# Other homes in SBUF for the tensors of a two-block transformer kernel on one core

## The chip, the core and the metric

The kernel runs on one core of a Trainium2 chip. TensorE does the matrix products, ScalarE and VectorE prepare operands and do the pointwise work, GpSimd takes small pieces and a few transfers, and SyncE issues the loads of the weights. The metric is the device time of one execution in microseconds (us); three runs of the kernel before gave 1877.51, 1879.15 and 1881.04 us.

SBUF, the memory on the chip, has 128 partitions. A tensor has the same start address in each partition. That start is called its home here, in bytes of the partition.

## The reference

Two blocks run one after the other on 256 rows of 1024 columns, all in float32. The first has two layers, the second has one. What matters here are the large products:

```python
def first_block(...):
    for l in range(2):
        h = _swiglu(x, ffn_w1[l, 0], ffn_w3[l, 0], ffn_w2[l, 0])      # 1024 -> 2816 -> 1024
        x = _layernorm(ALPHA * x + 0.5 * h, ln_g[l, 0], ln_b[l, 0])
        h = _mixer(x, l, w_in[l], ..., w_branch[l], w_out[l], cos, sin)  # 1024 -> 7168, attention, -> 1024
        x = _layernorm(ALPHA * x + h, ln_g[l, 1], ln_b[l, 1])
        h = _swiglu(x, ffn_w1[l, 1], ffn_w3[l, 1], ffn_w2[l, 1])
        x = _layernorm(ALPHA * x + 0.5 * h, ln_g[l, 2], ln_b[l, 2])
    return x

def second_block(...):
    h = modulate(rmsnorm(x, norm1_g), sh1, sc1)
    z = h @ w_in                                  # 1024 -> 5152, neighbourhood and linear attention
    y = sigmoid(m_a) * (o_na @ w_br_na) + sigmoid(m_b) * (o_gla @ w_br_gla)
    x = x + g1 * (y @ w_out)
    h2 = modulate(rmsnorm(x, norm2_g), sh2, sc2)
    return x + g2 * swiglu(h2, w_ffn_gate, w_ffn_up, w_ffn_down)
```

## The kernel before, in words

**Weights.** SyncE loads the weight matrices in chunks of 1 MB into three buffers `raw`. Each chunk is cut into two parts of 128 by 1024 numbers. ScalarE copies a part from `raw` to one of four buffers `whi` in the type fp32r, which rounds it (L1357), and VectorE writes the remainder `raw - whi` to one of four buffers `wlo` (L1821). The activations are split in the same way into a high and a low tensor.

**Products.** Each product is done as three matmuls: high times high, low times high, high times low. There are two forms.
- `gemm_a` (L671, L672, L674): the weight part is the stationary operand, 128 columns at a time, and the activations are the moving operand, 256 columns (1 KB of a partition). L671 holds `whi` and streams the high activations, L672 holds `whi` and streams the low ones, L674 holds `wlo` and streams the high ones. Each line is issued equally often. A group is eight steps of the contraction, 24 matmuls into one half of a PSUM bank.
- `gemm_b` (L694, L696, L697): the activations are the stationary operand and the weight part is the moving one, 512 columns (2 KB).

**Activations.** In the first block they are in `XTh` and `XTl` for most products, in `HCh` and `HCl` for the products with `w_branch`, and in `ffn1Hh`, `ffn1Hl` (or `ffn3...`) for the second matrix of the feed-forward part. In the second block they are in `HCh` and `HCl` everywhere but for the last matrix, which reads `ffn4Hh` and `ffn4Hl`.

**Order.** The order of every engine's instructions is written out by hand and does not depend on the homes. The queues are: SyncE's for the weights, GpSimd's for biases, tables and small inputs.

**Homes.** `sb` and `some` ask for tensors one after the other, and the allocator lays them down in that order, each size rounded up to 32 bytes, the first one at 16,512 bytes. Tensors in an `ExitStack` that is closed give their place back to the next ones. Worked out from the sizes, these are the starts modulo 1024 bytes, before and after the change:

| tensor | role | before | after |
|---|---|---|---|
| `raw` | landing of the loads | 128 | 0 |
| `whi`, `wlo` | stationary in `gemm_a`, moving in `gemm_b` | 128 | 0 |
| `XTh`, `XTl` | moving in `gemm_a`, stationary in `gemm_b` | 704 | 0 |
| `HCh`, `HCl` | the same, second block and branches | 736 | 0 |
| `ffn1Hh`, `ffn1Hl`, `ffn3Hh`, `ffn3Hl` | stationary in `gemm_b` | 416 | 0 |
| `ffn4Hh`, `ffn4Hl` | moving in `gemm_a` | 192 | 0 |
| `X`, `gb`, `csa`, `c2`, `QNT`, `KNT`, `V2` | attention, norm | 704 | 0 |
| `G2`, `LA`, `VG`, `NP`, `NPT` and others of the second block | attention | 192 | 512 |

Steps inside these tensors are multiples of 512 bytes (a `whi` part in `gemm_a` steps by 512 bytes per contraction step, `XTh` by 1 KB, `HCh` by 2 KB), so the remainder modulo 64 holds for every operand of a product: it was 0 for `whi`, `wlo`, `XTh`, `XTl`, `ffn4Hh`, `ffn4Hl` and 32 for `HCh`, `HCl`, `ffn1Hh`, `ffn1Hl`, `ffn3Hh`, `ffn3Hl`. The distances between a high tensor and its low one stay: 8 KB for `XT`, 16 KB for `HC`, 22 KB for `ffn4`.

Of the kernel before, what the change touches and what calls it, by code (L numbers as in the profile page):

```python
# [9 lines left out]
F32R = mybir.dt.float32r  # L10
# [19 lines left out]
C_ID, C_SHARED, C_CM = 0, 128, 128  # L30
# [320 lines left out]
def program(nc, I, out):  # L351
    ctx = ExitStack()

    def sb(stack, name, shape, dt=F32):
        return stack.enter_context(nc.sbuf_tensor(name, list(shape), dt))

    def some(stack, name, n, shape, dt=F32):
        return [sb(stack, f"{name}{i}", shape, dt) for i in range(n)]
# [4 lines left out]
    with ctx:  # L363
# [20 lines left out]


        bank = [ctx.enter_context(nc.psum_tensor(f"bank{i}", [128, 512], F32)) for i in range(8)]
        raw = some(ctx, "raw", 3, [128, 2048])
        whi = some(ctx, "whi", 4, [128, 1024], F32R)
        wlo = some(ctx, "wlo", 4, [128, 1024], F32R)
        cst = sb(ctx, "cst", [128, C_SHARED])  # L390
        cols = sb(ctx, "cols", [128, 128])
        modc = sb(ctx, "modc", [128, 48, 2])
        c4 = sb(ctx, "c4", [128, 8, 4], F32R)
        spare = sb(ctx, "spare", [128, 512])
        cmb = sb(ctx, "cmb", [4, 2])
        half = sb(ctx, "half", [128, 16])
        XTf = sb(ctx, "XTf", [128, 8, T])
        HCh = sb(ctx, "HCh", [128, 8, 512], F32R)
        HCl = sb(ctx, "HCl", [128, 8, 512], F32R)
        csil = sb(ctx, "csil", [128, 8, 2])  # L400
        sh = sb(ctx, "sh", [128, 48, 2])
        g1c = sb(ctx, "g1c", [128, 8, 2])
        g2c = sb(ctx, "g2c", [128, 8])
        sv2 = sb(ctx, "sv2", [128, 112])
        ident = cst[:, C_ID:C_ID + 128]
        rows = spare[:, 0:128]
        nhalf = half[:, 0:1]

        xst = ExitStack()
# [6 lines left out]
        mv = sb(xst, "mv", [128, 2, 2])  # L416
        rs = sb(xst, "rs", [128, 2, 4])
        gbh = sb(xst, "gbh", [128, 16])
        cm, cos, sin, perm = csa[:, 0:256], csa[:, 256:512], csa[:, 512:768], csa[:, 768:896]

        def ffn_bufs(st, name):
            return (sb(st, name + "Hh", [128, NF, T], F32R), sb(st, name + "Hl", [128, NF, T], F32R),
                    some(st, name + "S", 2, [128, T]), some(st, name + "Hf", 2, [128, T]))
# [64 lines left out]
        with ExitStack() as ns:  # L488
# [3 lines left out]
            NPT = some(ns, "NPT", 2, [128, 512])  # L492
            nv = some(ns, "nv", 3, [128, 8])
        with ExitStack() as fs:
            ffn4 = ffn_bufs(fs, "ffn4")
            OUT = sb(fs, "OUT", [128, 2, D])
        st.close()
# [2136 lines left out]
```

## Time and profile before

| | |
|---|---|
| three runs | 1877.51, 1879.15, 1881.04 us |
| the profiled execution | 1877.37 us, its span 1875.6 us |
| TensorE matmul busy | 1846.2 us, 98% of the span |
| VectorE busy | 1124.1 us, 60% |
| ScalarE busy | 890.9 us, 47% |
| loads | 330.58 MB, mean 176 GB/s |

The profiled execution lasted 1.8 us more than its span, the time from the first to the last instruction. The record of a matmul is longer than the distance to the next one, since matmuls are pipelined. So the busy time of TensorE says little. The pace is read from the distance between starts: in a stretch without a gap it is (length of the stretch + length of one record) / number of records that touch the stretch.

### The profile page before, as it was taken

To read this page: it belongs to the slowest core of one execution; us is meant where nothing else is said; L and a number is where in the kernel's file an instruction comes from. 1 tells how busy PE (TensorE), PEld (TensorE's weight loads), DVE (VectorE), ACT (ScalarE), POOL (GpSimd) and SP (SyncE) were. 2 spreads that over 40 slices of the span, in tenths; PEclk is the share of its full clock that TensorE was granted. 3 is DMA by queue.
4 is the path that set the end of the run, shared out by engine and by line. 5 is a ranking of instruction groups with operands and counts; after the bars stand their busy time and mean duration, and the time that the engine had idled before them with its cause. 6 is when DMAs were issued, how large, how long until landed. Compare 5 with 4: busy or idle time off the path is not lost.

```text
span 1875.6 us, 31147 instructions
## 1 busy us (share of the span) xinstructions
PE 1846.2 (98%) x12859; PEld 1649.6 (88%) x12859; DVE 1124.1 (60%) x1703; ACT 890.9 (47%) x1437; POOL 246.2 (13%) x261
## 2 busy tenths in 40 slices
PE   9999999999999999999999999999998999999999
PEld 8998699999899879986898997999776787879999
DVE  5654586676665465655675776566653645565553
ACT  5553344663455434543435753555344345454443
POOL 1000232111200020001321212000110712100000
PEclk9999999999999999999999999999998999999999
DMA  8665655445666566754745455665444223356553
GB/s 282 193 201 192 227 180 167 148 149 189 203 189 213 184 203 193 231 203 157 254 156 178 136 180 200 214 215 180 157 130 129 90 81 101 113 165 192 183 181 112
DMA packets 252397, 330.58 MB, mean 176 GB/s; under 512 B 13162, under 2 KB 213072, under 8 KB 252256
## 3 DMA queue, kind: packets, MB, share of 16 engines
q1 hardware_dynamic: 248240, 315.31, 52.3%
q0 software_dynamic: 4016, 13.27, 2.1%
q8 instruction: 102, 1.67, 0.4%
q14 instruction: 39, 0.32, 0.1%
HBM read 327.51 MB, written 1.05 MB: 175 GB/s over the span
## 4 chain that ended last, share of the span: by engine, by line
PE 64%; issue 23%; DVE 5%; DMA 3%; POOL 2%; ACT 2%; SPq 1%; DVEq 0%; POOLq 0%; ACTq 0%
PE bank L671 15%; PE bank L672 15%; PE bank L674 15%; PE bank L694 4%; PE bank L696 4%; PE bank L697 4%; DMA G<-in_lam_dram 1%; DVE X L1893 1%; DVE wlo L1821 1%; PE bank L1227 1%; DMA raw<-in_w_in_dram 1%; SPq L640 1%; POOL rs L2416 1%; PE bank L1205 1%; ACT whi L1357 1%
## 5 line engine op out<-in xcount | busy, mean ns | idle before, releaser
L1821 DVE TENSOR_TENSOR wlo<-raw,whi 128x1024 fp32r<-128x1024 f32 (+1 forms) x557 | 686.4, 1238 | 427.7 <-ACT whi L1357 424.9
L1357 ACT ACTIVATE whi<-raw 128x1024 fp32r<-128x1024 f32 (+1 forms) x569 | 594.4, 1051 | 430.3 <-PE bank L674 179.7
L671 PE MATMUL bank<-XTh,whi 128*128 128x256 f32 x2048 | 581.1, 284 | 2.0 <-DVE XTl L1830 2.0
L672 PE MATMUL bank<-XTl,whi 128*128 128x256 f32 x2048 | 572.3, 279 | 0.0
L674 PE MATMUL bank<-XTh,wlo 128*128 128x256 f32 x2048 | 571.9, 279 | 0.0
L671 PEld LDWEIGHTS bank<-XTh,whi 128*128 128x128 f32 x2048 | 384.3, 188 | 7.1 <-DVE XTl L1830 2.7
L672 PEld LDWEIGHTS bank<-XTl,whi 128*128 128x128 f32 x2048 | 384.6, 188 | 1.4
L674 PEld LDWEIGHTS bank<-XTh,wlo 128*128 128x128 f32 x2048 | 383.8, 187 | 0.0
L671 PE MATMUL bank<-HCh,whi 128*128 128x256 f32 (+1 forms) x936 | 272.9, 292 | 8.0 <-ACT whi L1357 5.8
L674 PE MATMUL bank<-HCh,wlo 128*128 128x256 f32 (+1 forms) x936 | 268.4, 287 | 0.0
L672 PE MATMUL bank<-HCl,whi 128*128 128x256 f32 (+1 forms) x936 | 268.0, 286 | 0.0
L671 PEld LDWEIGHTS bank<-HCh,whi 128*128 128x128 f32 x936 | 177.1, 189 | 25.6 <-issue 11.5
L672 PEld LDWEIGHTS bank<-HCl,whi 128*128 128x128 f32 x936 | 176.9, 189 | 2.1
L674 PEld LDWEIGHTS bank<-HCh,wlo 128*128 128x128 f32 x936 | 176.0, 188 | 2.8 <-DVE wlo L1821 0.8
L2416 POOL TENSOR_TENSOR rs<-rs,half 128x1 f32<-128x1 f32 x12 | 18.3, 1525 | 674.2 <-DVE rs L1887 674.2
L697 PE MATMUL bank<-whi,ffn1Hl 128*128 128x512 f32 x264 | 104.4, 396 | 0.0
L694 PE MATMUL bank<-whi,ffn1Hh 128*128 128x512 f32 x264 | 104.4, 395 | 0.0
L696 PE MATMUL bank<-wlo,ffn1Hh 128*128 128x512 f32 x264 | 104.4, 395 | 0.0
L694 PE MATMUL bank<-whi,XTh 128*128 128x512 f32 x192 | 76.2, 397 | 0.0
L697 PE MATMUL bank<-whi,XTl 128*128 128x512 f32 x192 | 75.8, 395 | 0.0
L696 PE MATMUL bank<-wlo,XTh 128*128 128x512 f32 x192 | 75.8, 395 | 0.0
L697 PEld LDWEIGHTS bank<-whi,ffn1Hl 128*128 128x128 f32 x264 | 49.6, 188 | 12.0
(329 smaller groups left out, 2316.0 us busy)
## 6 DMA issues: line engine op xcount, KB each, us to landing
raw<-in_ffn_w_dram SPq DMA_DIRECT2D x131, 1024.0 KB, 5.3
raw<-in_w_in_dram SPq DMA_DIRECT2D x76, 1024.0 KB, 5.2
raw<-in_w_mod_dram SPq DMA_DIRECT2D x24, 1024.0 KB, 5.1
raw<-in_w_branch_dram SPq DMA_DIRECT2D x16, 1024.0 KB, 5.1
raw<-in_w_out_dram SPq DMA_DIRECT2D x12, 1024.0 KB, 5.0
raw<-in_w_ffn_gate_dram SPq DMA_DIRECT2D x11, 1024.0 KB, 5.3
raw<-in_w_ffn_up_dram SPq DMA_DIRECT2D x11, 1024.0 KB, 5.3
raw<-in_w_ffn_down_dram SPq DMA_DIRECT2D x8, 1024.0 KB, 5.2
```

The lines of the kernel that those rows point to most:

```text
L640: e.dma_start(BT[64 * j:64 * j + 64, h, :, :], src).then_inc(BIAS[h].did(h, by=16), 16)
L671: e.matmul(o, hi[:, k, w0:w0 + nc_], xh, start=first and k == 0, stop=False)
L672: e.matmul(o, hi[:, k, w0:w0 + nc_], xl, start=False, stop=False)
L674: m = e.matmul(o, lo[:, k, w0:w0 + nc_], xh, start=False, stop=last and k == nk - 1)
L694: e.matmul(o[:, :], xh, hi[:, k, s], start=kk == 0, stop=False)
L696: e.matmul(o[:, :], xh, lo[:, k, s], start=False, stop=False)
L697: m = e.matmul(o[:, :], xl, hi[:, k, s], start=False, stop=kk == nparts * nk - 1)
L1205: e.matmul(bank[b][:, :], QNT[r, h // 2, t * 128:(t + 1) * 128], KNT[r, h // 2, :], start=True, stop=True).then_inc(SMALL.did(("ns", u)), 1)
L1227: m = e.matmul(o, V2[:, j, h * 64:(h + 1) * 64], NPT[u % 2][:, j * 128:(j + 1) * 128], start=j == 0, stop=j == 3)
L1357: e.activation(hi_part(n), raw_part(n), ACTF.Copy).then_inc(WHI.did(n), 1)
L1821: e.tensor_tensor(lo_part(n), raw_part(n), hi_part(n).bitcast(F32), ALU.subtract).then_inc(WLO.did(n), 1)
L2416: e.tensor_tensor(rs[:, t, 1:2], rs[:, t, 0:1], nhalf, ALU.pow).then_inc(PLN.did(("rs", j, t)), 1)
```

## The change

The order in which the shared tensors are asked for is another. `cst` and `modc` (896 bytes together) come first and fill the way up to 17,408 bytes, which is 17 KB. Then follow `raw`, `whi`, `wlo`, `XTf`, `HCh`, `HCl` and `spare`, whose sizes are multiples of 1 KB, then the small ones. Three tensors that nobody reads or writes (`gap0` 320 bytes, `gap1` 272, `gap2` 512) pad up to the next multiple of 1 KB ahead of `X`, of the buffers of the first block's stages, and of `ffn4`. Nothing else changes: the lists of instructions of all engines are the same, row for row, but for the line numbers, which grow by 2 to 4 behind the edits.

```diff
@@ -384,24 +384,26 @@
         bank = [ctx.enter_context(nc.psum_tensor(f"bank{i}", [128, 512], F32)) for i in range(8)]
+
+        cst = sb(ctx, "cst", [128, C_SHARED])
+        modc = sb(ctx, "modc", [128, 48, 2])
         raw = some(ctx, "raw", 3, [128, 2048])
         whi = some(ctx, "whi", 4, [128, 1024], F32R)
         wlo = some(ctx, "wlo", 4, [128, 1024], F32R)
-        cst = sb(ctx, "cst", [128, C_SHARED])
-        cols = sb(ctx, "cols", [128, 128])
-        modc = sb(ctx, "modc", [128, 48, 2])
-        c4 = sb(ctx, "c4", [128, 8, 4], F32R)
-        spare = sb(ctx, "spare", [128, 512])
-        cmb = sb(ctx, "cmb", [4, 2])
-        half = sb(ctx, "half", [128, 16])
         XTf = sb(ctx, "XTf", [128, 8, T])
         HCh = sb(ctx, "HCh", [128, 8, 512], F32R)
         HCl = sb(ctx, "HCl", [128, 8, 512], F32R)
+        spare = sb(ctx, "spare", [128, 512])
+        cols = sb(ctx, "cols", [128, 128])
+        sh = sb(ctx, "sh", [128, 48, 2])
+        c4 = sb(ctx, "c4", [128, 8, 4], F32R)
+        half = sb(ctx, "half", [128, 16])
         csil = sb(ctx, "csil", [128, 8, 2])
-        sh = sb(ctx, "sh", [128, 48, 2])
         g1c = sb(ctx, "g1c", [128, 8, 2])
         g2c = sb(ctx, "g2c", [128, 8])
         sv2 = sb(ctx, "sv2", [128, 112])
+        cmb = sb(ctx, "cmb", [4, 2])
+        sb(ctx, "gap0", [128, 80])
@@ -416,6 +418,7 @@
         gbh = sb(xst, "gbh", [128, 16])
+        sb(xst, "gap1", [128, 68])
@@ -492,6 +495,7 @@
         with ExitStack() as fs:
+            sb(fs, "gap2", [128, 128])
             ffn4 = ffn_bufs(fs, "ffn4")
```

## Rows read from the trace of the kernel before

**Rows 1.** The page: engines, busy us, share, instructions; then the granted clock.
```profile
PE 1846.2 (98%) x12859; PEld 1649.6 (88%) x12859; DVE 1124.1 (60%) x1703; ACT 890.9 (47%) x1437; POOL 246.2 (13%) x261
PEclk9999999999999999999999999999998999999999
```

**Rows 2.** The page: the chain that ended last, by engine, then by line.
```profile
PE 64%; issue 23%; DVE 5%; DMA 3%; POOL 2%; ACT 2%; SPq 1%; DVEq 0%; POOLq 0%; ACTq 0%
PE bank L671 15%; PE bank L672 15%; PE bank L674 15%; PE bank L694 4%; PE bank L696 4%; PE bank L697 4%; DMA G<-in_lam_dram 1%; DVE X L1893 1%; DVE wlo L1821 1%; PE bank L1227 1%; DMA raw<-in_w_in_dram 1%; SPq L640 1%; POOL rs L2416 1%; PE bank L1205 1%; ACT whi L1357 1%
```

**Rows 3.** Waits of the PE engine: total us, times, longest us.
```profile
PE bank L671 <- ACT whi L1357: 5.8, 1, 5.8
PE bank L696 <- DVE wlo L1821: 3.8, 2, 3.1
PE bank L732 <- DVE X L1893: 3.1, 5, 0.7
...
PE bank L732 <- DMA X<-in_x_dram: 1.1, 1, 1.1
...
PE bank L1152 <- DVE QD L2204: 0.9, 1, 0.9
```

**Rows 4.** Instruction groups by form: shape, count, busy us, mean ns, idle before.
```profile
L671 PE MATMUL bank<-XTh,whi 128*128 128x256 f32 x2048 | 581.1, 284 | 2.0 <-DVE XTl L1830 2.0
...
L671 PE MATMUL bank<-HCh,whi 128*128 128x256 f32 x912 | 261.4, 287 | 2.2 <-DVE HCl L2242 1.7 <-DVE tmp L2306 0.4
...
L694 PE MATMUL bank<-whi,ffn1Hh 128*128 128x512 f32 x264 | 104.4, 395 | 0.0
...
L694 PE MATMUL bank<-whi,XTh 128*128 128x512 f32 x192 | 76.2, 397 | 0.0
...
L671 PE MATMUL bank<-ffn4Hh,whi 128*128 128x256 f32 x176 | 49.5, 281 | 0.0
```

**Rows 5.** Stretches: us, busy (x records) per engine, granted clock, DMA share, GB/s.
```profile
500.00:550.00 50.00, 50.00 (x427) 50.00 (x426) 27.90 (x35) 24.35 (x36) 0.00 (x0) 1.00 0.61 191
1180.00:1220.00 40.00, 40.00 (x342) 40.00 (x341) 23.27 (x29) 20.10 (x29) 0.00 (x0) 1.00 0.65 204
1700.00:1800.00 100.00, 100.00 (x836) 100.00 (x835) 56.70 (x71) 49.36 (x71) 0.00 (x0) 1.00 0.58 182
1105.00:1125.00 20.00, 20.00 (x169) 20.00 (x169) 13.45 (x20) 9.88 (x13) 4.99 (x6) 1.00 0.59 201
1830.00:1865.00 35.00, 35.00 (x300) 35.00 (x299) 16.18 (x17) 13.52 (x15) 0.00 (x0) 1.00 0.41 130
150.00:200.00 50.00, 50.00 (x216) 40.24 (x215) 22.52 (x22) 17.47 (x18) 0.00 (x0) 1.00 0.56 189
```

**Rows 6.** Timeline of PE, one group of XTh: 21 matmuls lie between these two.
```profile
361.32 0.28 PE L672 MATMUL bank<-XTl,whi 128*128 128x256 f32 x1
...
363.81 0.28 PE L674 MATMUL bank<-XTh,wlo 128*128 128x256 f32 x1
```

**Rows 7.** A stretch of 512-column matmuls on HCh at half clock.
```profile
1425.00:1427.00 2.00, 2.00 (x6) 1.58 (x5) 1.97 (x4) 1.95 (x4) 0.29 (x1) 0.50 0.73 193
```

**Rows 8.** Timeline of PE there: 8 matmuls of 512 columns lie between these two.
```profile
1423.75 0.63 PE L671 MATMUL bank<-HCh,whi 128*128 128x512 f32 x1
...
1427.59 0.58 PE L671 MATMUL bank<-HCh,whi 128*128 128x512 f32 x1
```

**Rows 9.** Groups by form: one operation on ffn1 (home 416) and ffn4 (home 192).
```profile
L1853 DVE TENSOR_TENSOR ffn1Hl<-ffn1Hf,ffn1Hh 128x256 fp32r<-128x256 f32 x66 | 28.1, 425 | 31.9 <-ACT ffn1Hh L1391 31.9
...
L1391 ACT ACTIVATE ffn1Hh<-ffn1Hf 128x256 fp32r<-128x256 f32 x66 | 27.6, 418 | 39.2 <-DVE ffn1Hf L1850 39.2
...
L1853 DVE TENSOR_TENSOR ffn4Hl<-ffn4Hf,ffn4Hh 128x256 fp32r<-128x256 f32 x22 | 9.4, 425 | 10.6 <-ACT ffn4Hh L1391 10.6
...
L1391 ACT ACTIVATE ffn4Hh<-ffn4Hf 128x256 fp32r<-128x256 f32 x22 | 9.2, 418 | 11.9 <-DVE ffn4Hf L1850 11.9
```

**Rows 10.** DMA issues: count, size, median us from issue to landing.
```profile
raw<-in_ffn_w_dram SPq DMA_DIRECT2D x131, 1024.0 KB, 5.3
```

## Prediction

> **What bounds the kernel now.** I read the page first: TensorE's records cover 98% of the span, VectorE's 60%, ScalarE's 47%, at a clock that is at its upper level (2.4 GHz) nearly throughout [rows 1]. Then the chain: 64% of it is TensorE and 23% is "issue", and the three lines of `gemm_a` and the three of `gemm_b` lead it [rows 2]. Then the waits of TensorE: the longest is 5.8 us, and the others are a few us each [rows 3]. So the time is the number of matmuls times their distance, and a change of homes matters if it changes that distance. The instruction lists are the same, so no wait is added or taken away by the program.
>
> **The distance between matmuls.** All stretches used here have matmuls without a gap, and I divide (stretch + one record) by the records.
> - `XTh`, `XTl` streamed, 256 columns: (50 + 0.28) / 427 = 117.75 ns and (40 + 0.28) / 342 = 117.78 ns [rows 5].
> - `HCh`, `HCl` streamed, 256 columns: (100 + 0.28) / 836 = 119.95 ns and (20 + 0.28) / 169 = 120.0 ns [rows 5]. The first is in the second block, the second in the first block's branch products, so it isn't the stage.
> - `ffn4Hh`, `ffn4Hl` streamed: (35 + 0.28) / 300 = 117.6 ns [rows 5].
> - `whi`, `wlo` streamed, 512 columns: (50 + 0.395) / 216 = 233.3 ns [rows 4, 5].
>
> At 2.4 GHz, 256 columns are 106.7 ns and 512 are 213.3 ns. So each kilobyte costs some 10 to 13 ns more than its columns. At the lower clock this extra is gone: nine steps in 3.84 us are 426.7 ns, exactly 512 columns at 1.2 GHz [rows 7, 8]. I conclude that at the upper clock the reading of the operands sets the distance, and not the array. That makes the homes worth a look. The pace isn't set by transfers or other engines: 130 GB/s and 204 GB/s, ScalarE busy 39% and 50% of the stretch, give the same 117.6 to 117.8 ns [rows 5].
>
> The records themselves show the same difference: 284 ns for `XTh`, 281 for `ffn4Hh`, 287 for `HCh` [rows 4].
>
> **The change part by part.**
>
> *The streamed `HCh`, `HCl` (home 736, after 0).* What sets them apart from `XT` (704) and `ffn4` (192) is that they start at 32 modulo 64 bytes, where the others start at 0. The distance from the high to the low tensor does not sort them: it is 8 KB for one fast pair and 22 KB for the other. Nor does the stationary operand, which is `whi` or `wlo` at 128 in all. After the change they start at a multiple of 64. I take for them the pace of `XT`: 119.95 - 117.75 = 2.2 ns less per matmul. They are 912 on each of three lines [rows 4], 2736 in all: 2736 x 2.2 ns = 6.0 us. Not all of it reaches the end. Two groups (48 matmuls) run ahead of the 5.8 us wait for `whi`, whose part comes from a load, and four groups (96) run ahead of the 0.9 us wait for `QD` [rows 3]. A faster TensorE only waits longer there: 144 x 2.2 ns = 0.3 us is lost. That leaves 5.7 us. Bounds: nothing, if the 32 bytes aren't the reason; and 2736 x (119.95 - 113.2) = 18.5 us, if they fall to the best pace that the trace has (below).
>
> *The streamed `XT` and `ffn4` (704 and 192, after 0).* 3 x 2048 + 3 x 176 = 6672 matmuls. Both homes are 192 modulo 512, so the trace has only one start of this form at the good pace, and a start at 0 modulo 512 isn't shown. The nearest row says 117.75 ns, and I take no change. The bounds are wide. One group of `XTh` runs at (363.81 - 361.32) / 22 = 113.2 ns [rows 6], at the same addresses as all the others. In the timeline I count ten such groups of 256, all among the gates of the two mixers (361 to 389 and 1040 to 1069 us), each behind small matmuls of the attention; the other 246 are at 117.8. So a group falls into one of two rhythms by how it starts, and keeps it. Another home could tip all of them either way: 6672 x (117.75 - 113.2) = 30.4 us less, or, at the pace of `HC`, 6672 x 2.2 = 14.7 us more.
>
> *The streamed `whi`, `wlo` in `gemm_b` (128, after 0).* 233.3 ns whether the stationary operand is `ffn1` (home 416, 32 modulo 64) or `XT`: the records are 395 and 397 ns [rows 4]. At 512 columns the stationary home doesn't count, and the moving one already starts at a multiple of 128 bytes. I take nothing. Bound: the part that depends on the operand reading is 233.3 - 213.3 = 20 ns on each of some 1970 matmuls (264 and 192 on each of three lines [rows 4], and some 200 more on each), but no row has a 512-column stream at the upper clock without it, so I keep nothing for it beyond the tails.
>
> *Stationary operands.* In `gemm_a` the `whi` slices step by 512 bytes, so half of them started at 128 and half at 640, and go to 0 and 512. In the timeline the pace does not alternate with them. Nothing.
>
> *ScalarE, VectorE, GpSimd.* The same operations on `ffn1` (32 modulo 64) and `ffn4` (0) take 418 and 418 ns, 425 and 425 ns [rows 9]. Nothing, and both have idle time in any stretch [rows 5].
>
> *Loads.* `raw` moves from 128 to 0. A chunk of 1 MB lands 5.3 us after its issue [rows 10], and a chunk is used up in 48 x 117.75 ns = 5.65 us, with three buffers. If landing changed by a tenth either way, 0.5 us would show at the two waits that end with a load, for `X` (1.1 us) and for `whi` (5.8 us) [rows 3]: at most 1 us more or less. I take nothing. At `HC`'s new pace a chunk is needed every 5.65 us instead of 5.76, which `XT` stretches already bear.
>
> **The sum.** 1877.37 us (the profiled execution) - 5.7 = 1871.7 us. The median of the three runs lies 1.8 us above the profiled execution, which would make it 1873.4. I say 1872.
>
> **The Trainium skill against it.** The trace shows 120.0 ns for starts at 32 modulo 64 and 117.75 for starts at 0 modulo 64 [rows 5]. The Trainium skill, "SBUF — State Buffer", section "Specifications (TRN2)", gives lines of 16 bytes that need two hits or more for full bandwidth. By that rule every home before was at the start of a line already, a run of floats hits each line four times, and the change is worth nothing: 1877.4. It does not explain the 2.2 ns, so I follow the row, but it is one reason for the chance that I leave to no effect. The Trainium skill, "TensorE: Matmul & The Clock Gate", section "Step-by-step: what each phase is for", says that moving and stationary operands come through two independent read ports. By that rule an equal start of both operands cannot hurt, and rival three falls away. The two rhythms at one set of addresses [rows 6] speak for some coupling, and no row tells whether it is this one.
>
> **The rivals.**
> 1. *No effect.* `HC` is slow for another reason than the 32 bytes, for instance that its pair is 16 KB apart, just as `whi` and `wlo` are, or that its slices step by 2 KB. All this stays. Against it: the product rows show no other common trait of `XT` and `ffn4`. Time: 1877.4.
> 2. *The fast rhythm everywhere.* With both operands at full kilobytes all 256-column groups run at 113.2 ns. For it: the rhythm exists at unchanged addresses [rows 6]. Against it: no back-to-back group has it. Time: 1877.4 - 30.4 - 18.5 = 1828.5.
> 3. *Slower: the two operands of a matmul meet.* Before, moving and stationary starts differed by 64 modulo 512 for `XT` (704 - 128 = 576) and `ffn4` (192 - 128 = 64), and by 96 for `HC`. After, they differ by 0 everywhere. If both reads then fall on the same place at the same time, `XT` and `ffn4` go to the slow rhythm of 119.95 ns and `HC` stays: 1877.4 + 14.7 = 1892.1. It decides wherever 256-column groups run back to back, from the first feed-forward part on. For it: the difference sorts the streams as well as the 32 bytes do. Against it: its order is not monotone in any way that I can read.
>
> **How the numbers follow.** The forecast gets 0.50, no effect 0.19, the fast rhythm 0.17, the slower one 0.14. The forecast's own range is 1868 to 1875. The range for 8 in 10 holds the forecast, no effect and the slower rival, and leaves out the fast rhythm (0.17): 1864 to 1893. About 0.2%, 3.8 us, can be told from no change by a measurement of this kernel. Faster by more: 0.47 of the forecast's 0.50 and all of the fast rhythm, 0.64. Within: 0.03 and 0.19, 0.22. Slower: 0.14.
>
> **What would show it.** Right: stretches of `HC` at 117.8 ns, that is 851 records in a stretch of 100 us instead of 836, and the record of `HCh` 3 ns shorter; 427 records in 50 us of `XT` as before; 216 in 50 us of the 512-column form. The records of ScalarE and VectorE keep their means. The forecast is wrong if `HC` stays at 836 (first rival), if `XT` goes to 444 (second) or to 419 (third), or if the 512-column form leaves 233.3 ns, which none of my cases has.

## The result, and the profile after: slower by 0.23%

The changed kernel takes 1882.75 us (median of 13 runs, 1880.81 to 1884.3), the one before 1878.0 us (13 runs, 1875.0 to 1881.04). The ratio is 1.0023, with a 95% interval of 1.0015 to 1.0032: slower, by little more than a measurement can tell. I had forecast 1872 us. The time lies in my range and the sign is wrong. Of all the timed executions in this document one, of the kernel w128 below, took 2225.67 us at a granted clock of 0.75, and no ratio includes it.

The profiled span is 1881.5 us (before 1875.6). Lines behind the edits are 4 higher, so `gemm_a` is L675, L676 and L678, and `gemm_b` is L698, L700 and L701. The page's first line and the shares of its chain are those of [rows 1, 2] but for a point:

```profile
PE 1849.3 (98%) x12859; PEld 1664.8 (88%) x12859; DVE 1125.6 (60%) x1703; ACT 890.5 (47%) x1437; POOL 245.4 (13%) x261
...
PE 64%; issue 23%; DVE 5%; DMA 3%; POOL 2%; ACT 2%; SPq 1%; DVEq 0%; POOLq 0%; ACTq 0%
```

What moved is in the groups of instructions with their shapes (busy time, then the mean of one in ns):

```profile
L675 PE MATMUL bank<-XTh,whi 128*128 128x256 f32 x2048 | 589.4, 288 | 2.0 <-DVE XTl L1834 2.0
...
L675 PE MATMUL bank<-HCh,whi 128*128 128x256 f32 x912 | 262.6, 288 | 2.2 <-DVE HCl L2246 1.7 <-DVE tmp L2310 0.4
...
L698 PE MATMUL bank<-whi,ffn1Hh 128*128 128x512 f32 x264 | 102.7, 389 | 0.0
...
L698 PE MATMUL bank<-whi,XTh 128*128 128x512 f32 x192 | 75.2, 392 | 0.0
...
L675 PE MATMUL bank<-ffn4Hh,whi 128*128 128x256 f32 x176 | 50.1, 284 | 0.0
```

The streamed activations are longer (`XTh` 284 to 288 ns, `ffn4Hh` 281 to 284, `HCh` 287 to 288), the streamed weights shorter (395 to 389 on `ffn1`, 397 to 392 on `XTh`) [rows 4]. A record holds more than the distance to the next, so the size is read from counts: records of TensorE in a stretch without a gap. The rows are `XT`, `HC`, the 512-column form on `ffn1`, and `ffn4`:

```profile
500.00:550.00 50.00, 50.00 (x419) 50.00 (x418) 27.92 (x35) 24.01 (x34) 0.00 (x0) 1.00 0.58 184
1700.00:1780.00 80.00, 80.00 (x669) 80.00 (x669) 45.17 (x56) 39.10 (x56) 0.00 (x0) 1.00 0.59 185
150.00:190.00 40.00, 40.00 (x178) 33.14 (x177) 17.81 (x15) 15.66 (x15) 0.00 (x0) 1.00 0.58 192
1825.00:1850.00 25.00, 25.00 (x211) 25.00 (x210) 13.04 (x14) 9.42 (x11) 0.00 (x0) 1.00 0.60 192
```

(Stretch + one record) / records gives 50.28 / 419 = 120.0 ns for `XT` (before 117.75), 80.28 / 669 = 120.0 for `HC` (before 119.95), 40.39 / 178 = 226.9 for the 512-column form (before 233.3), 25.28 / 211 = 119.8 for `ffn4` (before 117.6) [rows 5]. One record more or less makes 0.3 ns in 50 us of `XT`, 0.6 ns in 25 us of `ffn4` and 1.3 ns in 40 us of the 512-column form. So both signs of being wrong have come: 419 records in 50 us, which I had named for my third rival, and 512-column matmuls off 233.3 ns, which I had said none of my cases has.

The three longest waits of TensorE stand in the same order as before, and the wait for `G` has moved up to the fourth place:

```profile
PE bank L675 <- ACT whi L1361: 6.9, 1, 6.9
PE bank L700 <- DVE wlo L1825: 4.0, 2, 3.3
PE bank L736 <- DVE X L1897: 3.9, 5, 0.8
...
PE bank L844 <- POOL G L2432: 2.2, 2, 1.6
```

The first three were 5.8, 3.8 and 3.1 us [rows 3]. The one for `G` was 1.1 us:

```profile
PE bank L840 <- POOL G L2428: 1.1, 2, 0.6
```

**Where the time went**, as number times change of distance:

| stream | matmuls | ns each | us |
|---|---|---|---|
| `XT`, 256 columns | 6144 | +2.25 | +13.8 |
| the ten groups that ran at 113.2 ns | 240 | +4.5 beyond that | +1.1 |
| `ffn4`, 256 columns | 528 | +2.2 | +1.2 |
| `HC`, 256 columns | 2736 | 0 | 0 |
| weights on `ffn1`, `ffn3`, 512 columns | 1056 | -6.6 | -7.0 |
| weights on `XT`, 512 columns | 576 | -6.4 | -3.7 |
| weights on `HC`, 512 columns | 336 | about -8 | -2.7 |
| waits for `whi`, for `G` and for `X` | | | about +3 |

They add up to some +6, and the spans differ by 5.9 us. The row on `HC` with 512 columns is read from the starts of its matmuls in both traces, where 84.5 us became 81.8; the mean change there holds more than the pace, since few of these matmuls run long without a break. The rows come from one profiled execution of each, and the runs of a kernel spread by 3 to 6 us, so I don't press the last microsecond. Two effects of opposite sign nearly cancel: +16 us on 256 columns and -13 us on 512.

ScalarE and VectorE keep their durations, as forecast [rows 9]:

```profile
L1395 ACT ACTIVATE ffn1Hh<-ffn1Hf 128x256 fp32r<-128x256 f32 x66 | 27.6, 418 | 36.5 <-DVE ffn1Hf L1854 36.5
...
L1857 DVE TENSOR_TENSOR ffn1Hl<-ffn1Hf,ffn1Hh 128x256 fp32r<-128x256 f32 x66 | 28.1, 425 | 31.9 <-ACT ffn1Hh L1395 31.9
```

### The profile page after: what moved, and what is told of

It reads as the page before. It is cut to its first block, busy times and chain, and to the rows that moved or that the text cites. A ratio compares the mean times of both kernels' runs of the same rounds, so it can differ in the third digit from the quotient of the medians.

```text
span 1881.5 us, 31147 instructions
## 1 busy us (share of the span) xinstructions
PE 1849.3 (98%) x12859; PEld 1664.8 (88%) x12859; DVE 1125.6 (60%) x1703; ACT 890.5 (47%) x1437; POOL 245.4 (13%) x261
## 4 chain that ended last, share of the span: by engine, by line
PE 64%; issue 23%; DVE 5%; DMA 3%; POOL 2%; ACT 2%; SPq 1%; DVEq 0%; POOLq 0%; ACTq 0%
PE bank L675 15%; PE bank L678 15%; PE bank L676 15%; PE bank L698 4%; PE bank L700 4%; PE bank L701 4%; DMA G<-in_lam_dram 1%; DVE X L1897 1%; DMA raw<-in_w_in_dram 1%; DVE wlo L1825 1%; PE bank L1231 1%; SPq L644 1%; POOL rs L2420 1%; ACT whi L1361 1%; PE bank L1209 1%
## 5 line engine op out<-in xcount | busy, mean ns | idle before, releaser
L675 PE MATMUL bank<-XTh,whi 128*128 128x256 f32 x2048 | 589.4, 288 | 2.0 <-DVE XTl L1834 2.0
L676 PE MATMUL bank<-XTl,whi 128*128 128x256 f32 x2048 | 579.9, 283 | 0.0
L678 PE MATMUL bank<-XTh,wlo 128*128 128x256 f32 x2048 | 579.9, 283 | 0.0
L675 PEld LDWEIGHTS bank<-XTh,whi 128*128 128x128 f32 x2048 | 392.2, 191 | 7.1 <-DVE XTl L1834 2.7
L676 PEld LDWEIGHTS bank<-XTl,whi 128*128 128x128 f32 x2048 | 392.2, 192 | 1.4
L678 PEld LDWEIGHTS bank<-XTh,wlo 128*128 128x128 f32 x2048 | 392.2, 191 | 0.0
L675 PE MATMUL bank<-HCh,whi 128*128 128x256 f32 (+1 forms) x936 | 274.2, 293 | 9.1 <-ACT whi L1361 6.9
L678 PE MATMUL bank<-HCh,wlo 128*128 128x256 f32 (+1 forms) x936 | 269.1, 288 | 0.0
L676 PE MATMUL bank<-HCl,whi 128*128 128x256 f32 (+1 forms) x936 | 269.0, 287 | 0.0
L675 PEld LDWEIGHTS bank<-HCh,whi 128*128 128x128 f32 x936 | 179.8, 192 | 27.2 <-issue 12.1
L678 PEld LDWEIGHTS bank<-HCh,wlo 128*128 128x128 f32 x936 | 179.6, 192 | 2.7 <-DVE wlo L1825 0.8
L676 PEld LDWEIGHTS bank<-HCl,whi 128*128 128x128 f32 x936 | 180.0, 192 | 2.1
L698 PE MATMUL bank<-whi,ffn1Hh 128*128 128x512 f32 x264 | 102.7, 389 | 0.0
L700 PE MATMUL bank<-wlo,ffn1Hh 128*128 128x512 f32 x264 | 102.7, 389 | 0.0
L701 PE MATMUL bank<-whi,ffn1Hl 128*128 128x512 f32 x264 | 102.7, 389 | 0.0
L698 PE MATMUL bank<-whi,XTh 128*128 128x512 f32 x192 | 75.2, 392 | 0.0
L700 PE MATMUL bank<-wlo,XTh 128*128 128x512 f32 x192 | 74.8, 390 | 0.0
L701 PE MATMUL bank<-whi,XTl 128*128 128x512 f32 x192 | 74.7, 389 | 0.0
L1393 ACT ACTIVATE ffn1S<-bank 128x256 f32<-128x256 f32 x66 | 25.3, 384 | 77.0 <-PE bank L678 77.0
```

Source lines behind the costliest of these rows:

```text
L675: e.matmul(o, hi[:, k, w0:w0 + nc_], xh, start=first and k == 0, stop=False)
L676: e.matmul(o, hi[:, k, w0:w0 + nc_], xl, start=False, stop=False)
L678: m = e.matmul(o, lo[:, k, w0:w0 + nc_], xh, start=False, stop=last and k == nk - 1)
L698: e.matmul(o[:, :], xh, hi[:, k, s], start=kk == 0, stop=False)
L700: e.matmul(o[:, :], xh, lo[:, k, s], start=False, stop=False)
L701: m = e.matmul(o[:, :], xl, hi[:, k, s], start=False, stop=kk == nparts * nk - 1)
```

## The experiments

Theory B of the recorded expectations: the distance between matmuls follows from the *difference* of the two homes that one matmul reads, start of the streamed operand minus start of the held one, modulo some power of two (512 in the first expectations, 256 in the later ones). My own theory of the prediction (A) was that the streamed home alone counts. All kernels below change homes only: the order in which tensors are asked for, and tensors that nobody uses as padding. "Home" is the start modulo 1024 bytes. Before: weights 128, `XT` 704, `HC` 736, `ffn1` and `ffn3` 416, `ffn4` 192. `raw`, `whi` and `wlo` always start alike, but in one kernel.

**w0** puts the weights at 0 and leaves the activations at 704, 736, 416 and 192. **w128** does the reverse: weights stay at 128, the activations go to 0.

```diff
 (w0, against before)
+        cst = sb(ctx, "cst", [128, C_SHARED])
+        modc = sb(ctx, "modc", [128, 48, 2])
         raw = some(ctx, "raw", 3, [128, 2048])
         whi = some(ctx, "whi", 4, [128, 1024], F32R)
         wlo = some(ctx, "wlo", 4, [128, 1024], F32R)
-        cst = sb(ctx, "cst", [128, C_SHARED])
+        XTf = sb(ctx, "XTf", [128, 8, T])
         cols = sb(ctx, "cols", [128, 128])
-        modc = sb(ctx, "modc", [128, 48, 2])
...
 (w128, against before)
...
         gbh = sb(xst, "gbh", [128, 16])
+        sb(xst, "pad2", [128, 72])
...
+            sb(fs, "pad4", [128, 208])
             ffn4 = ffn_bufs(fs, "ffn4")
```

> Only the weight parts move: raw, whi, wlo start at 0 modulo 1024 as after the change, XT stays at 704, HC at 736, ffn1 and ffn3 at 416, ffn4 at 192 as before it. Theory A (the pace of a matmul depends on the start of its moving operand alone): 256-column matmuls as before, 117.8 ns on XT and ffn4 and 120.0 on HC; 512-column matmuls, which stream the weight parts, 226.7 ns as after. Time 1878.0 - 12 = 1866 us. Theory B (it depends on the difference of the two starts): XT - weights was 64 modulo 512 and is 192, so XT leaves 117.8, and the 512-column matmuls have three new differences (416, 704, 736) and would not all run at 226.7. Time 1876 to 1893 us.

> The other half of the change: the weight parts stay at 128 as before, XT, HC, ffn1, ffn3, ffn4 start at 0. Theory A (own start of the moving operand): all 256-column matmuls 120.0 ns, 512-column ones 233.3 ns, time 1878.0 + 15 = 1893 us. Theory B (difference of the starts, here 384 modulo 512 for all): the 256-column pace is something else than 120.0, or the 512-column pace something else than 233.3.

w0: 1852.21 against 1878.94 us, ratio 0.9852 (0.9836 to 0.9868). w128: 1880.77 us, ratio 1.001 (1.0 to 1.0019). No time expected for w0 came true: A had 1866 us and B 1876 to 1893. Nor did A's 1893 us for w128. In w0 the stretches of `XT`, `HC` and the 512-column form on `ffn1` are

```profile
480.00:545.00 65.00, 65.00 (x576) 65.00 (x575) 38.12 (x47) 33.82 (x48) 0.00 (x0) 1.00 0.69 222
1700.00:1780.00 80.00, 80.00 (x678) 80.00 (x677) 45.79 (x57) 39.44 (x56) 0.00 (x0) 1.00 0.59 186
150.00:190.00 40.00, 40.00 (x173) 32.16 (x172) 17.15 (x14) 15.63 (x15) 0.00 (x0) 1.00 0.58 192
```

and in w128

```profile
500.00:550.00 50.00, 50.00 (x423) 50.00 (x423) 28.49 (x35) 24.70 (x35) 0.00 (x0) 1.00 0.57 175
1700.00:1780.00 80.00, 80.00 (x676) 80.00 (x676) 45.54 (x56) 39.66 (x58) 0.00 (x0) 1.00 0.60 185
150.00:190.00 40.00, 40.00 (x174) 32.43 (x173) 17.24 (x15) 15.21 (x15) 0.00 (x0) 1.00 0.54 185
```

`XT` has not moved in w0 and goes from 117.75 to 65.28 / 576 = 113.3 ns, which is the fast rhythm of [rows 6], now in some 220 of its 256 groups. `HC` hasn't moved either and goes from 119.95 to 80.28 / 678 = 118.4 ns. The 512-column form, which streams the weights that moved, stays at 40.39 / 173 = 233.5 ns, where A asked for 226.7. So the held operand's home counts, and A is out. In w128 the home of `HC` is a multiple of 64, and it doesn't take 117.75 ns but 80.28 / 676 = 118.8. In the changed kernel, with the same home 0 and the weights at 0, it took 120.0. Both homes count.

**s1, s2** tell apart a difference and two separate effects. The homes are these: s1 has weights 0, `XT` 64, `HC` 128, `ffn1` 32; s2 has weights 64, `XT` 64, `HC` 128, `ffn1` 0. The edits are paddings and an order near that of the changed kernel. The paddings in the first block, of s1:

```diff
 (s1, against before)
         gb = sb(xst, "gb", [128, 2, D])
+        sb(xst, "pad1", [128, 96])
         XTh = sb(xst, "XTh", [128, 8, T], F32R)
...
         gbh = sb(xst, "gbh", [128, 16])
+        sb(xst, "pad2", [128, 64])
...
```

> Sweep, weight parts at 0. XT at 64, HC at 128, ffn4 at 512, ffn1 and ffn3 at 32. Theory A: 512-column matmuls stay at 226.7 ns whatever the stationary start; the 256-column pace is read for three new starts; 512 (ffn4) should equal 0 and give 120.0 if the pattern repeats every 512 bytes, and 64 or 128 should give 117.8 if it is the distance from such a boundary that helps. Theory B: XT has the difference 64 that it had before, so it runs at 117.8; the 512-column pace differs between ffn1 (difference 32) and XT (64).

> Sweep, weight parts at 64. XT at 64, HC at 128, ffn4 at 256, ffn1 and ffn3 at 0. Theory A: XT (64) and HC (128) run at the same pace as in the run with weight parts at 0 and the same homes; the 512-column pace is that of a stream that starts at 64, a new value between 226.7 and 240. Theory B: XT (difference 0) runs at 120.0, HC (difference 64) at 117.8, and both differ from the other sweep.

Both are single executions: 1876.6 and 1878.44 us. Stretches of s1, then of s2:

```profile
500.00:550.00 50.00, 50.00 (x427) 50.00 (x426) 28.17 (x35) 24.11 (x35) 0.00 (x0) 1.00 0.62 191
1700.00:1780.00 80.00, 80.00 (x676) 80.00 (x676) 45.54 (x56) 39.40 (x56) 0.00 (x0) 1.00 0.59 186
```

```profile
500.00:550.00 50.00, 50.00 (x419) 50.00 (x419) 27.94 (x35) 24.11 (x34) 0.00 (x0) 1.00 0.60 183
1700.00:1780.00 80.00, 80.00 (x681) 80.00 (x681) 46.08 (x58) 39.72 (x57) 0.00 (x0) 1.00 0.60 185
150.00:190.00 40.00, 40.00 (x176) 32.84 (x175) 18.28 (x15) 14.82 (x14) 0.00 (x0) 1.00 0.57 197
```

`XT` at home 64 has 427 records with the weights at 0 (difference 64) and 419 with the weights at 64 (difference 0). 427 is the count of before, where the homes were 704 and 128, and the difference 64 as well modulo 256. `HC` in s2 has difference 64 too, at 80.28 / 681 = 117.9 ns; in s1 it has 128 and 118.8 ns, w128's value at its difference 128. The third row of s2, 512 columns with weights minus held at 64, has 40.39 / 176 = 229.5 ns, where 224 and 192 had 233.3 and 0 had 226.9. The difference sorts all of them.

**best** sets what the rows so far make the best: difference 192 for all 256-column streams, and 0 for the weights on `ffn1` and `ffn3`. **shift32** is best with every home 32 bytes further, so that nothing starts at a multiple of 64 and all differences stay.

```diff
 (best, against w0)
-        cols = sb(ctx, "cols", [128, 128])
         c4 = sb(ctx, "c4", [128, 8, 4], F32R)
         half = sb(ctx, "half", [128, 16])
-        g2c = sb(ctx, "g2c", [128, 8])
         HCh = sb(ctx, "HCh", [128, 8, 512], F32R)
         HCl = sb(ctx, "HCl", [128, 8, 512], F32R)
         spare = sb(ctx, "spare", [128, 512])
+        cols = sb(ctx, "cols", [128, 128])
...
+        g2c = sb(ctx, "g2c", [128, 8])
...
         gbh = sb(xst, "gbh", [128, 16])
+        sb(xst, "pad1", [128, 152])
 (shift32, against best)
         modc = sb(ctx, "modc", [128, 48, 2])
+        g2c = sb(ctx, "g2c", [128, 8])
...
         gb = sb(xst, "gb", [128, 2, D])
+        sb(xst, "pad1", [128, 8])
...
```

> Weight parts at 0, XT at 704, HC and ffn4 at 192, ffn1 and ffn3 at 0 modulo 1024. Theory B (the pace depends on the moving start minus the stationary start, modulo 256): 256-column matmuls have 192 everywhere and run at 113.3 ns, HC too (it was 118.3 with weight parts at 0 and HC at 736); the 512-column ones on ffn1 and ffn3 have 0 and run at 226.7 (233.3 there). Against the kernel with only the weight parts moved, 1852 us: 2661 x 5.0 ns = 12 us and 1048 x 6.7 ns = 7 us less, about 1833 us. Theory A (own start of the moving operand): HC goes to what 192 gave in ffn4, also 113.3, but the 512-column pace cannot depend on the home of ffn1 and stays 233.3: about 1840 us.

> All homes of the kernel with weight parts at 0, XT at 704, HC and ffn4 at 192, ffn1 and ffn3 at 0 moved up by 32 bytes, so that nothing starts at a multiple of 64 and all differences stay. Theory B (differences alone): the same paces, 113.3 ns and 226.7 ns on ffn1. The step of my prediction (32 modulo 64 costs 2.2 ns): 256-column matmuls 2 ns or more longer on all of XT, HC and ffn4.

best: 1839.86 us (1832.58 to 1844.64) against 1879.02, ratio 0.9793 (0.9765 to 0.9821). It is faster than before, by 2.1% (1.8 to 2.4). Against the changed kernel, not timed beside it, the medians give 1839.86 / 1882.75 = 0.977. shift32: 1836.71 us, one execution. In best, an early stretch of `XT`, a later one, `HC`, and the 512-column form:

```profile
480.00:545.00 65.00, 65.00 (x576) 65.00 (x575) 38.73 (x49) 35.12 (x49) 0.00 (x0) 1.00 0.63 202
...
680.00:735.00 55.00, 55.00 (x469) 55.00 (x469) 31.83 (x40) 27.80 (x40) 0.00 (x0) 1.00 0.61 190
...
1700.00:1780.00 80.00, 80.00 (x708) 80.00 (x707) 47.62 (x58) 41.20 (x59) 0.00 (x0) 1.00 0.58 184
150.00:190.00 40.00, 40.00 (x179) 33.10 (x178) 17.48 (x15) 14.85 (x14) 0.00 (x0) 1.00 0.57 187
```

and in shift32 `HC` and the 512-column form:

```profile
1700.00:1780.00 80.00, 80.00 (x708) 80.00 (x707) 47.04 (x58) 40.06 (x57) 0.00 (x0) 1.00 0.62 195
150.00:190.00 40.00, 40.00 (x178) 33.12 (x177) 18.11 (x15) 14.85 (x14) 0.00 (x0) 1.00 0.58 189
```

`HC` runs at 80.28 / 708 = 113.4 ns in both, 6.6 ns below the changed kernel. That no home of these operands is a multiple of 64 in shift32 costs nothing in these rows. The rows of `XT` in best show the two rhythms at one difference: 65.28 / 576 = 113.3 ns, and 55.28 / 469 = 117.9 ns over a stage. In the timeline 77 of `XT`'s 256 groups take the slow one in best, 40 in shift32, 34 to 36 in w0. Against w0 the 43 or so more slow groups are 43 x 24 x 4.44 ns = 4.6 us. Of `HC`'s 114 groups 17 are slow in best as well, another 17 x 24 x 4.44 ns = 1.8 us, and the waits are some 1.3 us longer. That is most of the 8.4 us by which the profiled execution (1841.45 us) misses the 1833 us that were expected. The runs of best spread over 12 us; whether that is the number of slow groups, one trace can't say. Back to back, a group nearly always keeps the rhythm of the one before it, so that most stages go one way; but in the first stage of w0 the fifth group changes and the eleven behind it stay slow. What picks the rhythm is open.

**nextld** asks whether what counts is the operand held *now* or the one being loaded for the next matmul. It is best with `wlo` at 64 and `XTl` at 768, so that the two differences of a matmul, to its own and to the next held operand, part.

```diff
 (nextld, against best)
         whi = some(ctx, "whi", 4, [128, 1024], F32R)
+        sb(ctx, "pad1", [128, 16])
         wlo = some(ctx, "wlo", 4, [128, 1024], F32R)
...
+        sb(xst, "pad2", [128, 240])
         XTh = sb(xst, "XTh", [128, 8, T], F32R)
+        sb(xst, "pad3", [128, 16])
         XTl = sb(xst, "XTl", [128, 8, T], F32R)
...
```

> As the kernel with weight parts at 0, XT at 704, HC and ffn4 at 192, ffn1 and ffn3 at 0, but wlo starts at 64 and XTl at 768, each 64 bytes further; whi and XTh stay. Theory N (a stream meets the load of the NEXT matmul's stationary operand, which runs beside it): the stream of XTl meets the load of wlo, difference 192 modulo 256, the two streams of XTh meet loads of whi, 192 too, so all three of XT stay at 113.3 ns; on HC and ffn4, whose low tensor did not move, the matmul that streams the low tensor gets 128 and takes longer, the other two stay. Theory O (a stream meets its OWN stationary operand): the low stream of XT has 0 and the high one with wlo 128, so XT goes to about 118 ns in the mean; on HC and ffn4 the matmul with wlo gets longer, the one that streams the low tensor doesn't.

1877.61 us, one execution: all of the gain is gone.

```profile
500.00:550.00 50.00, 50.00 (x425) 50.00 (x424) 28.47 (x34) 23.56 (x33) 0.00 (x0) 1.00 0.60 190
1700.00:1780.00 80.00, 80.00 (x679) 80.00 (x679) 45.52 (x56) 39.91 (x57) 0.00 (x0) 1.00 0.60 187
150.00:190.00 40.00, 40.00 (x175) 32.34 (x174) 17.22 (x15) 15.28 (x15) 0.00 (x0) 1.00 0.56 185
```

`XT` is at 118.3 and `HC` at 118.2 ns. From the paces measured above, the own held operand (theory O) asks for (113.3 + 120.0 + 118.8) / 3 = 117.4 ns on `XT` and (113.3 + 113.3 + 118.8) / 3 = 115.1 ns on `HC`. The next one (theory N) asks for 113.3 and 115.1. N fails clearly on `XT`, and both are some 3 ns short on `HC`. On `ffn1` either would have (226.7 + 226.7 + 229) / 3 = 227.5 ns, and the row has 40.39 / 175 = 230.8. So the paces don't add up over the three matmuls of a step: differences that change from one matmul to the next cost more than their mean. Which of the two held operands counts stays open.

**s3** and **s4** read the table at more differences: s3 has weights 0, `XT` 32, `HC` 160, `ffn1` 256, `ffn4` 448. s4 has weights 0, `ffn1` 0, `ffn4` 32, and puts `XT` at 688 and `HC` at 208 by beginning 16 bytes inside a larger tensor.

```diff
 (s4, against w0)
...
-        XTh = sb(xst, "XTh", [128, 8, T], F32R)
-        XTl = sb(xst, "XTl", [128, 8, T], F32R)
+        sb(xst, "pad1", [128, 240])
+        XTb = sb(xst, "XT", [128, 16 * T + 8], F32R)[:, 4:4 + 16 * T].rearrange("p (k t) -> p k t", k=16)
+        XTh, XTl = XTb[:, 0:8, :], XTb[:, 8:16, :]
...
 (s3, against w0)
...
+        sb(xst, "pad1", [128, 88])
         XTh = sb(xst, "XTh", [128, 8, T], F32R)
...
```

> Sweep of the difference, weight parts at 0: XT 32, HC 160, ffn4 448; ffn1 and ffn3 at 256. Theory B with period 256: ffn4 (448 = 192 + 256) at 113.3 ns, ffn1 (difference 0 modulo 256) at 226.7 ns, the 512-column XT (224) at 233.3; XT at 32 and HC at 160 are new points, expected between 113.3 and 120. With period 512 instead, ffn4 and ffn1 differ from that.

> Finer sweep in steps of 16 bytes, weight parts at 0: XT at 688 (difference 176 modulo 256), HC at 208, ffn4 at 32, ffn1 and ffn3 at 0. 192 had two rhythms, 113.3 and 117.8 ns; the question is whether 176 or 208 hold the fast one in all groups. The theory of differences expects ffn4 at 116.8 (what XT had at 32) and ffn1 at 226.7, and XT and HC between 113.3 and 118.5; over 118.5 would be against it.

One execution each: 1866.77 and 1879.56 us. In s3 `XT` (in a good stretch; from 500 to 550 us it has 419 records, which is 120.0 ns), `HC`, `ffn4`, and the 512-column form:

```profile
1180.00:1220.00 40.00, 40.00 (x345) 40.00 (x344) 23.95 (x30) 20.77 (x30) 0.00 (x0) 1.00 0.58 183
1700.00:1780.00 80.00, 80.00 (x677) 80.00 (x676) 45.73 (x57) 39.43 (x57) 0.00 (x0) 1.00 0.59 185
1825.00:1850.00 25.00, 25.00 (x223) 25.00 (x222) 13.37 (x15) 10.46 (x11) 0.00 (x0) 1.00 0.45 146
150.00:190.00 40.00, 40.00 (x178) 33.15 (x177) 18.36 (x15) 15.22 (x15) 0.00 (x0) 1.00 0.59 200
```

and in s4 `XT`, `HC` and `ffn4`:

```profile
500.00:550.00 50.00, 50.00 (x422) 50.00 (x421) 28.25 (x35) 24.62 (x34) 0.00 (x0) 1.00 0.57 180
1700.00:1780.00 80.00, 80.00 (x673) 80.00 (x673) 45.52 (x56) 39.33 (x57) 0.00 (x0) 1.00 0.58 185
1825.00:1850.00 25.00, 25.00 (x217) 25.00 (x216) 12.23 (x13) 9.66 (x11) 0.00 (x0) 1.00 0.68 220
```

s3 sets the modulus at 256: `ffn4` at 448 runs at 25.28 / 223 = 113.4 ns, as at 192, and the 512-column form on `ffn1` at 256 at 40.39 / 178 = 226.9 ns, as at 0. In s4 `XT` at difference 176 takes 50.28 / 422 = 119.1 ns, and `HC` at 208 takes 80.28 / 673 = 119.3 ns. I had written that more than 118.5 would speak against the theory of differences with a cost that falls evenly toward 192, and it does speak against the even fall. These are also the only two homes off the multiples of 32 bytes, so nothing tells whether the differences 176 and 208 are dear or the odd 16 bytes.

**xt640, hc704, ffn128** change one home of the kernel before each: `XT` from 704 to 640 (difference 64 to 0), `HC` from 736 to 704 (96 to 64, which is just the step that my forecast rests on), `ffn1` and `ffn3` from 416 to 128 (weights minus `ffn1` from 224 to 0).

```diff
 (xt640)
+        sb(xst, "pad1", [128, 240])
         XTh = sb(xst, "XTh", [128, 8, T], F32R)
         XTl = sb(xst, "XTl", [128, 8, T], F32R)
+        sb(xst, "pad2", [128, 16])
 (hc704)
-        cmb = sb(ctx, "cmb", [4, 2])
         half = sb(ctx, "half", [128, 16])
...
         g2c = sb(ctx, "g2c", [128, 8])
+        cmb = sb(ctx, "cmb", [4, 2])
 (ffn128)
         gbh = sb(xst, "gbh", [128, 16])
+        sb(xst, "pad1", [128, 184])
```

> The kernel before with XTh and XTl alone moved from 704 to 640, so that their difference to the weight parts (128) is 0 modulo 256, as after the whole change. The theory of differences: XT at 120.0 ns instead of 117.8 (6144 matmuls, +14 us), the 512-column matmuls that hold XT at 226.7 ns instead of 233.3 (576, -4 us), all others as before: about 1889 us against 1879. If instead the start at a full kilobyte were what hurts, 640 would do as well as 704 and nothing would change.

> The kernel before with HCh and HCl alone moved from 736 to 704: the step that I predicted by itself (-5.7 us). The theory of differences: 576 - that is 64 modulo 256, the difference that XT has in the kernel before - gives 117.8 ns on 2736 matmuls instead of 120.0, so 6 us less, 1873 us against 1879, and nothing in the 512-column form. If HC is slow for a reason of its own (pair 16 KB apart, steps of 2 KB), nothing changes.

> The kernel before with the stack of ffn1 and ffn3 alone moved from 416 to 128, so that the 512-column matmuls that stream whi and wlo over them have the difference 0. The theory of differences: 226.7 ns instead of 233.3 on 1056 matmuls, 7 us less, about 1872 us. If the stationary home does not count, as my prediction had it, no change.

| kernel | time, us | ratio to before | 95% interval |
|---|---|---|---|
| xt640 | 1887.83 | 1.0044 | 1.003 to 1.0058 |
| hc704 | 1873.03 | 0.9966 | 0.9955 to 0.9978 |
| ffn128 | 1871.6 | 0.9961 | 0.9948 to 0.9974 |

The times that theory B had named were 1889, 1873 and 1872 us. Each kernel moves its own stream, with one side effect: in hc704 13 of the 20 groups of `ffn4`, whose homes stayed, ran in the fast rhythm, which is worth 1.5 us in its trace. The `XT` stretch of xt640, the `HC` stretch of hc704 and the 512-column stretch of ffn128:

```profile
500.00:550.00 50.00, 50.00 (x419) 50.00 (x419) 28.23 (x34) 24.35 (x34) 0.00 (x0) 1.00 0.56 178
```

```profile
1700.00:1780.00 80.00, 80.00 (x682) 80.00 (x681) 45.67 (x57) 39.78 (x57) 0.00 (x0) 1.00 0.60 185
```

```profile
150.00:190.00 40.00, 40.00 (x178) 33.15 (x177) 18.30 (x15) 15.28 (x15) 0.00 (x0) 1.00 0.59 200
```

They are 120.0, 117.7 and 226.9 ns. xt640 alone costs +9.6 us by the medians (1887.83 - 1878.21) and 0.44%, which is 8.3 us, by the ratio (5.6 to 10.9). ffn128 alone gives 6.6 us by the medians and 0.39%, 7.3 us, by the ratio, for the 1056 matmuls x 6.6 ns = 7.0 us of the table. These are the main parts of the two halves of the change. By the same sum xt640 ought to cost 13.8 + 1.1 = 14.9 us less a gain on its 512-column form, whose difference goes to 0 too (-3.7 us): 11.2, just above that interval. Its own trace has +13.5 and -3.5 us there, 10.0 in all.

## Why the prediction was wrong, step by step

- **What bounds the kernel** held: no wait appeared or went, and the time followed the distance between matmuls. So did the method of counting records. The clause that the reading of the operands sets the distance, and not the array, fits all that follows, but no run shows it.
- **The step on `HC` failed.** I read from two homes that a start at 32 modulo 64 bytes costs 2.2 ns and a start at 0 doesn't. I sorted by the streamed home alone and dismissed the weights with "whi or wlo at 128 in all". They were at 128 in all, and for that reason no row could tell a home from a difference. Against the first rival I wrote that the rows show no other common trait of `XT` and `ffn4`, and the third rival then names one. The difference of `HC` was 96, that of `XT` and `ffn4` 64. shift32 shows that 32 modulo 64 costs nothing. hc704, the step by itself, gave -0.34%, which is 6.4 us (5.2 by the medians), where I had 5.7, and in its trace the matmuls on `HC` take 5.7 us less: right in size by luck, for another reason. The change put `HC` at difference 0, where the pace is 120.0 ns, as it was at 96. Instead of -5.7 us, nothing.
- **"The nearest row says 117.75 ns, and I take no change"**, on `XT` and `ffn4`, failed as well: +2.2 ns each, the bound I had of 14.7 us upward, and measured at 15.0 (13.8 + 1.2), with another 1.1 us for the ten fast groups. My third rival named this cause, "both reads then fall on the same place", and I gave it 0.14, because it "is not monotone in any way that I can read". It needn't be: of its two rows, 64 and 96, one was good.
- **"At 512 columns the stationary home doesn't count"** failed: the homes of the held `ffn1` and `XT` gave differences (weights minus held) of 224 and 192, which both cost 233.3 ns, and I took two points that agree for a law. At 0 it is 226.7 ns. I bounded this by 20 ns a matmul and set it to zero, because no row had another value. It was 6.6 ns, and took back some four fifths of the loss. That is why the result is 1882.75 and not my third rival's 1892.1.
- **ScalarE, VectorE, half clock, waits**: nothing, as written. The waits for `whi`, `G` and `X` came out some 3 us longer in one execution. Nothing here tests whether that is the homes' doing; in w0, which runs faster, the first of them is 7.1 us.
- **Loads**: a chunk lands 5.1 us after its issue instead of 5.3 [rows 10], within the tenth that I had allowed, and no wait shows it.

The Trainium skill, "TensorE: Matmul & The Clock Gate", section "Step-by-step: what each phase is for", has moving and stationary operands come through two independent read ports. In w0 the streamed activations stayed where they were, and their pace changed with the home of the held weights, from 117.75 to 113.3 ns. So what the prediction drew from that rule, that an equal start of both can't hurt, is wrong here, and the measurement decides. Whether the two meet in the ports or elsewhere, no run shows.

## What to carry to other kernels

Where back-to-back matmuls stream one operand and load the next, read the distance between matmuls for each pair of operands (records in a stretch without a gap), and treat the two homes as a pair: here, of the eight differences tried in steps of 32 bytes, 192 modulo 256 was best for 256 columns and 0 for 512. Aligning everything to a large power of two makes all differences 0, which for 256 columns was as bad as any (120.0 ns, as at 96). When all rows share one home, they can't tell that home from a difference: give the rival that names the difference its full chance, and move one home at a time.

## What the runs showed of the hardware

Distance between matmuls at the granted clock of 1.00 (2.4 GHz), by start of the streamed minus start of the held operand, modulo 256 bytes, in ns; held operand 128 columns wide, both of fp32r:

| difference | 0 | 32 | 64 | 96 | 128 | 160 | 192 | 224 |
|---|---|---|---|---|---|---|---|---|
| 256 columns | 120.0 | 116.8 | 117.8 | 120.0 | 118.8 | 118.6 | 113.3 | 118.4 |
| 512 columns | 226.7 | 233.2 | 228.9 | 233.3 | 232.4 | 234.2 | 233.3 | 233.3 |

The 512-column values are distances between starts in groups of 24 matmuls; those at 32 and 160 come from 8 groups on `HC` each, in w0 and in the kernel before.

At 192, 113.3 is the fast rhythm and 117.8 the slow one. At 64 the usual pace was 117.8, and 113.3 in 10 of `XT`'s 256 groups before, in 34 of them in s1 and in 13 of `ffn4`'s 20 in hc704. Other differences have a second pace too: 120.0 ns in some 25 groups of `XT` at 32 (s3) and in 29 at 128 (w128), and some 117.2 ns in 44 of `HC`'s 114 groups at 160 (s3). The 512-column form at 64 took 233.3 instead of 228.9 ns in 4 of the 22 groups on `XT` in best, and in 13 in shift32. An equal mean can hide another pattern: at 96 the single distances of `HC` range from 116 to 125 ns, and at 0 nearly all are 120.

At 1.2 GHz nothing of it is left: exactly the columns [rows 7, 8], 426 or 427 ns for 512 in all fourteen traces. The matmuls with 32 or 4 columns held and 512 streamed have medians from 227 to 235 ns in the fourteen traces, without an order by the homes of the weights; that the full-width load takes part is a guess from this.

Landing of a 1 MB chunk also follows the home of `raw`: 5.1 us at 0 (seven kernels), 5.3 at 128 (five), 5.4 at 64 and at 32 (one each). In the changed kernel:

```profile
raw<-in_ffn_w_dram SPq DMA_DIRECT2D x131, 1024.0 KB, 5.1
```

Open are: what picks the rhythm, why 512 columns prefer 0 and 256 columns 192, and how the operand held and the one being loaded share in it.
